# Attention placed between the gate tiles of the input projection, sample logits and values in four column quarters, raw input turned, last expert's rows summed over six banks

## The reference

```python
h = rmsnorm(x, norm1_g)
z = h @ w_in      # u | q | k | v | indexer q, k, weights | gate_pool | gate_attn
pool_out = pool_mix(concat(pool_hist, u))          # windows 2, 4, 8, 16, then w_pool
q, k = rmsnorm(q, q_norm_g), rmsnorm(k, k_norm_g)
att = dsa_attention(q, qi, wi, k_all, v_all, ik_all)   # top keys by an indexer, bias, softmax
mixed = sigmoid(g_pool) * (pool_out @ w_branch_pool) + sigmoid(g_attn) * (att @ w_branch_attn)
x = x + mixed @ w_out
x = x + moe_ffn(rmsnorm(x, norm2_g))   # top 4 of 32 experts, clamped SwiGLU, 12.6 MB of weights each
```

## Time and profile before

| | |
|---|---|
| median of 3 runs | 1384.34 us (1380.25 to 1384.99) |
| the profiled execution | 1380.85 us, span 1379.0 us |
| PE busy | 1310.8 us, 95% |
| DVE, ACT, POOL busy | 430.8, 189.9, 34.4 us |
| moved by DMA | 443.14 MB, mean 321 GB/s |

### The profile page before, as it was taken

One profiled execution on the slowest core, in us unless ns is written; L12 is line 12 of the kernel. 1 busy time (PEld: TensorE's weight loads), 2 busy tenths in 40 slices (PEclk: granted clock), 3 DMA queues, 4 the chain that ended last, 5 costly groups with the idle time before them and its releaser, 6 DMA issues.

```text
span 1379.0 us, 15153 instructions
## 1 busy us (share of the span) xinstructions
PE 1310.8 (95%) x6011; PEld 578.0 (42%) x6011; DVE 430.8 (31%) x779; ACT 189.9 (14%) x361; POOL 34.4 (2%) x37
## 2 busy tenths in 40 slices
PE   5999997789899999999999999999999999999996
PEld 2435444765455434344343443434434344343422
DVE  1047004132143343322433223332233323333223
ACT  3121112230111110101101111011110101101000
POOL 4000004000000000000000000000000000000000
PEclk9999999889998999999999999999999999999998
DMA  9131231031626999999999999999999999999993
GB/s 320 62 122 62 95 120 63 1 130 62 261 102 239 367 428 429 428 428 429 428 428 430 427 429 430 426 430 429 427 430 429 427 429 429 428 430 428 428 430 135
DMA packets 45716, 443.14 MB, mean 321 GB/s; under 512 B 4931, under 2 KB 6747, under 8 KB 20606
## 3 DMA queue, kind: packets, MB, share of 16 engines
q1 hardware_dynamic: 41344, 434.93, 75.6%
q10 hardware_dynamic: 3054, 4.90, 1.0%
q0 software_dynamic: 1296, 2.99, 0.7%
HBM read 439.27 MB, written 3.53 MB: 321 GB/s over the span
## 4 chain that ended last, share of the span: by engine, by line
PE 77%; DMA 3%; DVE 2%; ACT 1%; issue 0%; SPq 0%; DVEq 0%; POOL 0%; PEldq 0%
PE bank L1494 33%; PE bank L1505 16%; PE bank L1514 7%; PE bank L1480 7%; PE bank L1351 3%; PE bank L1432 3%; PE bank L1556 2%; DMA ring<-in_w_down 2%; PE bank L1569 1%; DMA wpool<-in_w_pool 1%; PE bank L1363 1%; PE bank L1362 1%; PE bank L1333 1%; PE bank L1332 1%; DMA ring<-in_w_out 1%; ACT logit L614 1%
## 5 line engine op out<-in xcount | busy, mean ns | idle before, releaser
L1494 PE MATMUL bank<-ring,xT 128*64 128x512 f32 x2048 | 475.2, 600 | 1.0 <-DVE xT L1057 0.7
L1494 PEld LDWEIGHTS bank<-ring,xT 128*64 128x64 f32 x2048 | 132.8, 136 | 285.0 <-issue 278.4
L1505 PE MATMUL bank<-ring,aT 128*64 128x512 f32 x1024 | 227.7, 597 | 2.4 <-DMA ring<-in_w_down 2.4
L1081 DVE TENSOR_TENSOR x<-x,bank 128x512 f32<-128x512 f32 x198 | 127.2, 684 | 129.1 <-PE bank L1514 129.1
L1161 PE MATMUL bank<-ring,hT 128*128 128x512 f32 (+1 forms) x384 | 161.9, 582 | 2.2 <-DMA ring<-in_w_in 1.9
L1505 PEld LDWEIGHTS bank<-ring,aT 128*64 128x64 f32 x1024 | 72.4, 138 | 143.1 <-issue 138.6
L1514 PE MATMUL bank<-yS,back 64*128 64x512 f32 x396 | 112.8, 646 | 8.4 <-DVE x L1081 7.6
L1094 DVE TENSOR_TENSOR gz<-bank,bguT 128x512 f32<-128x512 f32 x64 | 41.2, 686 | 221.8 <-PE bank L1556 221.8
L1161 PEld LDWEIGHTS bank<-ring,hT 128*128 128x128 f32 x384 | 73.5, 193 | 86.8 <-issue 82.8
L1480 PEld LDWEIGHTS bank<-pick,h 128*128 128x128 f32 x768 | 88.8, 195 | 13.2 <-issue 13.2
L1480 PE MATMUL bank<-pick,h 128*128 128x128 f32 x768 | 91.8, 281 | 1.0 <-DVE pick L1013 1.0
(11 more groups left out here) (253 smaller groups left out, 783.4 us busy)
## 6 DMA issues: line engine op xcount, KB each, us to landing
ring<-in_w_gate_up SPq DMA_DIRECT2D x128, 2048.0 KB, 17.3
ring<-in_w_down SPq DMA_DIRECT2D x64, 2048.0 KB, 17.3
ring<-in_w_in SPq DMA_DIRECT2D x16, 1024.0 KB, 8.1
ring<-in_w_out SPq DMA_DIRECT2D x4, 1024.0 KB, 5.9
ring<-in_cache_k SPq DMA_DIRECT2D x2, 1024.0 KB, 6.7
ring<-in_cache_v SPq DMA_DIRECT2D x2, 1024.0 KB, 6.7
ring<-in_w_branch_pool SPq DMA_DIRECT2D x2, 1024.0 KB, 6.8
ring<-in_w_branch_attn SPq DMA_DIRECT2D x2, 1024.0 KB, 11.2
```

The costliest lines, as they stand in the source:

```text
L1081: V.tensor_tensor(x[:, t, 512 * h:512 * h + 512], x[:, t, 512 * h:512 * h + 512], bank[6 + h][:, :], ALU.add).then_inc(y_added, 1)
L1494: last = T.matmul(bank[j][64 * r:64 * r + 64, :], xT[:, w, SLOTS * a:SLOTS * a + SLOTS], src[:, FF * r + 512 * j:FF * r + 512 * j + 512], ...
L1505: last = T.matmul(bank[4][64 * r:64 * r + 64, :], aT[:, c, :], src[:, o:o + 512], start=(c == 0), stop=(c == KC - 1))
```

## The change

1. **Start.** SP issues the loads of x, the constants and then the weights, without waiting for x. POOL's loads wait for the first two weight units. PE turns the raw x; DVE multiplies by `norm1_g` while it copies `hT` out, and the inverse root is applied by ACT as the scale of each copy of a projection's sums. The first block runs in two halves of the contraction.
2. **Order.** Only the five blocks that feed the attention run as blocks (`DENSE`). The four gate blocks become twelve `gate_tile(k)`, one token tile each, in banks 6 and 7, and PE's list puts them between the steps of the attention. The ring's units are reordered to match; the stores of the new keys and values move from ACT's list to SP's. Gate columns are copied out plainly, and three Sigmoids over 2048 columns follow at the end.
3. **Samples.** `qblk` holds 32 columns per sample and head pair. Four matmuls with 32 columns each write rows 32c to 32c+31 of the bank. Values have turned probabilities (32 columns) as stationary operand and 128 columns of values as moving one, again four column quarters. Softmax's division moves behind the values (`rowS`), whose rows are then turned back (8 transposes).
4. **End.** The last expert's gates are turned in the middle of the expert before's `down`, its places ahead, and the rows of the last two experts are summed for all three token tiles in six banks, so that x is added to once. x is stored in three parts.

```diff
-            sp.wait_ge(x_in[NT - 1], 16)
+            for t in range(NT):
+                src = I["x_prompt"][0, t * P:(t + 1) * P, :] if t < 2 else I["x_sample"].rearrange("b s d -> (b s) d")
+                sp.dma_start(x[:, t, :], src).then_inc(x_in[t], 16)
...
+            pool.wait_ge(unit_in[0], 16)
+            pool.wait_ge(unit_in[1], 16)
...
-            pe.wait_ge(xn_ready, NT)
-            for c in range(KC):
-                for t in range(NT):
-                    last = T.transpose(bank[c][:, t * P:(t + 1) * P], xn[:, t, c::KC], ident)
+            for m in range(2 * NT):
+                t, hf = divmod(m, 2)
+                pe.wait_ge(x_in[t], 16)
+                for q in range(4):
+                    last = T.transpose(bank[m][:, q * P:(q + 1) * P], x[:, t, 4 * hf + q::KC], ident)
...
                 for m in range(4):
-                    out = bank[2 * r + m // 2]
+                    b = 4 * r + m
+                    out = bank[((4, 0), (1, 2))[r][m // 2]]
                     o = (m % 2) * 256
-
-                    T.matmul(out[:, o:o + 256], rep[:, 4 * r + m, :], neg[:, 2, :], start=True, stop=False)
+                    T.matmul(out[:, o:o + 256], rep[:, b, :], neg[:, 2, :], start=True, stop=False)
                     for c in range(PAIRS):
-                        T.matmul(out[:, o:o + P], qblk[:, m, c, :], kTs[:, m, c, :], start=False, stop=False)
-                        last = T.matmul(out[:, o + P:o + 256], qblk[:, m, c, :], kT[:, c, 2 * P:], start=False,
-                                        stop=(c == PAIRS - 1))
+                        T.matmul(out[32 * c:32 * c + 32, o:o + P], qblk[:, b, c, :], kTs[:, m, c, :], start=False, stop=False)
+                    for c in range(PAIRS):
+                        last = T.matmul(out[32 * c:32 * c + 32, o + P:o + 256], qblk[:, b, c, :], kT[:, c, 2 * P:],
+                                        start=False, stop=True)
...
+                        for own in range(2):
+                            for c in range(PAIRS):
+                                v = zv[:, 2, c * P:(c + 1) * P] if own else ring[:, (vc_u + r) % RING, m * 512 + c * P:m * 512 + (c + 1) * P]
+                                last = T.matmul(bank[4 + r][32 * c:32 * c + 32, m * P:(m + 1) * P],
+                                                pT[:, 2 * b + own, 32 * c:32 * c + 32], v, start=(own == 0), stop=(own == 1))
...
                     for w in range(4):
-                        down(place + (KC if more else 0) + w, i, w)
+                        if final and w == 2:
+                            pe.wait_ge(z_added, 2 * n + 2)
+                            turn_gates(n + 1)
+                        down(place + KC + w, i, w)
...
+            for t in range(NT):
+                combine_last(t, back, True)
+            pe.wait_ge(at_ready, n + 1)
+            for w in range(4):
+                down(KC + UNITS + w, turns, w, aT2)
+            pe.wait_ge(y_out, n + 2)
+            pe.wait_ge(back_ready, n + 2)
+            for t in range(NT):
+                combine_last(t, back2, False)
```

More of the change, by code:

```diff
@@ L502, in _ @@
             act.wait_ge(sumsq_done, NT)
+            act.wait_ge(root_set, 1)
             A.activation(rsx, ssx, ACT.Sqrt, bias=eps, scale=1.0 / D).then_inc(rms_done, 1)
[L505 to L512, removed]
+            act.wait_ge(rsx_ready, 1)
             def z_block(m):
@@ L730, in turn @@
             def turn(i, final):
-                for a in range(2):
+                for a in range(1 if final else 2):
                     n = 2 * i + a
@@ L750, in _ @@
             turn(turns, True)
+            units = turns * (2 * UNITS) + KC
+            sigmoid(turns * 2 + 2)
+            rows_out(units + UNITS)
+            act.wait_ge(back_turned, turns * 2 + 2)
+            A.activation(back2[:], bank[5][:, 0:TOK].rearrange("p (t q) -> p t q", t=NT), ACT.Copy).then_inc(back_ready, 1)
+            rows_out(units + (UNITS + 4))
         @block.vector
@@ L1165, in z_block @@
                 pe.sem_inc(released, 2)
-            z_block(0)
+            pe.wait_ge(ht_ready, 2 * NT)
+            for half in range(2):
+                unit_wait(pe, half)
+                for t in range(NT):
+                    for c in range(4 * half, 4 * half + 4):
+                        last = z_part(0, t, c)
+                    if half:
+                        last.then_inc(z_done, 1)
+            pe.wait_ge(z_done, NT)
+            pe.sem_inc(released, 2)
+            pe.wait_ge(relb_in, 32)
+            T.matmul(bank[6][0:H, 0:NREL], relb[:], onehot[:], start=True, stop=True).then_inc(pe_small, 1)
             pe.wait_ge(idx_in, 16)
@@ new lines, in turn_rows_back @@
+            def turn_rows_back():
+                for bb in range(2):
+                    pe.wait_ge(rows_ready, bb + 1)
+                    for m in range(4):
+                        last = T.transpose(bank[4 + bb][:, m * P:(m + 1) * P], rowS[:, 4 * bb + m, :], ident)
+                    last.then_inc(rows_turned, 1)
+            turn_heads(0)
+            gate_tile(0)
+            turn_heads(4)
+            gate_tile(1)
+            logits(0)
+            gate_tile(2)
+            turn_probs(0)
@@ new lines, in _ @@
+            logits(1)
+            gate_tile(3)
+            values(0)
+            gate_tile(4)
+            turn_probs(1)
+            gate_tile(5)
+            values(1)
+            turn_keys(0)
+            gate_tile(6)
+            cache_logits(0)
+            turn_keys(1)
+            gate_tile(7)
+            cache_logits(1)
+            gate_tile(8)
+            gate_tile(9)
+            turn_probs(2)
+            gate_tile(10)
+            cache_values()
+            pool_mix()
+            gate_tile(11)
```

552 lines of the change are left out of this document (298 added, 254 removed).

## The result

The changed kernel takes 1312.39 us (median of 4, 1310.48 to 1315.62) where the one before takes 1383.32: a ratio of 0.9501, interval 0.9485 to 0.9517. The forecast was 1313. The two profiled executions (1380.85 us before, 1315.62 after) lie at opposite ends of their kernels' runs, so their spans differ by 65.2 us only.

| from | to | before | after | gained | forecast |
|---|---|---|---|---|---|
| start | pool rows turned | 153.3 | 144.4 | 8.9 | 10 |
| there | last branch matmul | 201.6 | 154.7 | 46.9 | 50 |
| there | first `gate_up` | 73.0 | 73.5 | -0.5 | 0 |
| there | first wait for the last `w_down` is over | 911.6 | 913.1 | -1.5 | 0 |
| there | end | 39.5 | 28.1 | 11.4 | 11 |

The account below looks back on a forecast made before the run. PE, 95% busy, was taken as the bound, with PE and DMA limits together in the experts. Start 10, attention 50 and end 11 sum to 71: 1384.3 - 71 = 1313 us, range 1306 to 1320, chance 0.62.

Parts of the forecast that it names:

- Start, 10 us forecast: Kernel start: first block begins at 11.0 instead of 21.54 us, less 0.5 for the `rel_bias` matmul; 10 us gained.
- the second of the two times that were worked out: First block: turned x, with DVE's last copies, ready at 10.9 us; the other time, the weights', was 11.0.
- Attention, 50 forecast: Pool rows turned to end of branch matmuls: 201.6 us becomes 151.3, gate tiles covering the softmax; 50 us less.
- the gate tiles: Attention: twelve tiles, nine at 6.9 us (a third of a block) and three at 4.4, make 75.3 us.
- waits move: Rival: ACT, DVE or queues come late for some gate tiles, half of 22.5 us idle stays; 1324 us, chance 0.15.
- the halves were the right neighbour: Samples' matmuls: quarters behave as halves do, four run beside each other, so eight matmuls take 0.44 us.
- Starts: Rival, samples: starts at 0.068 us set the pace, a sample's 16 take 1.09 instead of 0.44; 1323 us, chance 0.10.
- no overlap: Rival, samples: quarters do not run beside each other, 1.74 us instead of 0.44; 1334 us, chance 0.06.
- the slower case: Rival, samples: every change of quarter empties the array, 128 matmuls at 0.78 us; 1406 us, chance 0.02.
- the estimate of 3.2: Samples: speed-up of four column tiles, estimated from the skill's 2.38 for three; a round 0.55 us, sum 1.7 longer.
- End, 11 forecast: Last two experts to the end: finish at 1367.5 in a span of 1379.0; 11 us, 7 if additions wait as before.
- the gain reaches the end: Expert stage moves forward whole; rival, transfers set the experts' pace and only the end's 11 us stay: 1373, chance 0.03.

Follow-up runs that it names:

- one_quarter: Changed kernel with half of the samples' quarter matmuls writing rows 0 to 31, so it computes another thing; 2261.45 us, including a second pass over the experts.
- quarter_runs: Changed kernel with the samples' two matmuls that write one quarter listed one behind the other, then the next quarter; 1311.16 us, 0.9486 of the kernel before.
- old_end: Changed kernel with all of the end as in the kernel before; 1325.59 us, 0.9585 of the kernel before.
- late_gates: Changed kernel with the last expert's gates turned behind the whole `down` of the expert before, not in its middle; 1317.04 us, 0.9523 of the kernel before.
- gates_first: Changed kernel with the first six gate tiles ahead of the attention instead of between its steps; 1334.59 us, 0.9660 of the kernel before.
- mended: Changed kernel with second logits earlier, sample masks paired, gated rows turned early and w_out begun on the weight units there; 1303.25 us, 0.9440 of the kernel before.

## Why the prediction was right

**Start, 10 us forecast, 8.9 in the pair of traces.** The block began at 12.0, not 11.0; it waited for DVE's last copy of the turned x, which is the second of the two times that were worked out, about 1 us later than that. Over the traces the u rows begin to turn at 138.6 to 142.5 (before: 150.7), 8.2 to 12.1 earlier. By the runs POOL's hold carries 5.6 us of it; the early issue isn't told from scatter. No run takes away the turning of the raw x, and it matters as well: by the earlier trace rows PE ended the transposes of `xn` at 13.38 + 4.62 = 18.0, so with `xn` as before the block could not have begun at 12.0, however early the weights came.

**Attention, 50 forecast, 46.9.** The pieces came out as summed: the samples' logits 9.4 (forecast 9.5), values with their end 4.0 (3.7), the branch matmuls 41.4 (41.2), logits and values of the prompt 6.0 (6.0). The term that was sized too small is the gate tiles: the twelve fill 77.0 us, not 75.3. They were costed as thirds of a block; a tile with other work behind it ends 0.1 to 0.3 later. Transposes made 12.0 instead of 11.4, waits 2.2 instead of 1.6. Beyond the 0.9 us that was counted, no wait for ACT appeared, and none for a weight unit or a queue, so "waits move" fell; that the tiles hide the softmax was shown by taking them away.

**Quarters.** Four beside each other, 0.22 for eight instructions, against 8 x 0.109 = 0.87 on one quarter: the halves were the right neighbour. "Starts" (1.09 for 16) and "no overlap" (1.74) fell with the period of 1.20 us, and so did the slower case, a drain at each change. That case was priced from masks that ran at full pace (0.21 us from one instruction of 256 columns to the next), so its price held no slow clock, though its words had one. The earlier trace rows shown as 0.07 us are a weak reading against starts 0.062 or 0.068 apart; a view of 0.02 us (224.01 to 224.03) still holds both starts, which settles it. The Trainium skill, TensorE: Matmul & The Clock Gate, Part 3, gives 2.38 for three column tiles at 512 columns. Here a sample's 16 instructions take 0.44 us on four quarters, and they would take 16 x 0.109 = 1.74 on one by the spacing in `one_quarter`, four times that; so the measurement decides against the estimate of 3.2. The same part of the Trainium skill says that matmuls start strictly in program order. The records of `quarter_runs` and `one_quarter` show otherwise for column quarters in fp32.

**End, 11 forecast, 11.4** in the pair and 12.1 by `old_end`. The places of the gain are the forecast ones; `late_gates` shows that the place of the turned gates carries 4.3 of it, more than the 1.2 that were counted there.

**The rest.** The two stages that were to stay lost 2.0 us together, in one trace. With 65.2 the traces give less than the 71 summed, and the medians 70.9. Of the gap of 5.7, 2.5 is that the profiled execution of before lies so far under its median, and 2.3 may be the slow first block (23.20 against 20.87), which most traces do not have; the last microsecond stays open. That the median came within 1 us is therefore luck in part; terms of 10, 50 and 11 that were each within 13% of what the traces show (8.9, 46.9 and 11.4) are not. That the gain reaches the end was shown three times: by the result, by `gates_first` and by `mended`, with 909 to 912 us from the first to the last `gate_up` in every trace but that of `one_quarter`.

## What to carry to other kernels

Independent work that stands in large blocks on the bounding engine was worth more here between the steps of a chain that waits for other engines: split it by the length of the waits (here 8.5 and 11.8 us, covered by tiles of 7), and count for each piece what a block pays once at its end (0.1 to 0.3 us). Before a step is moved, walk through the list of every engine that it passes: the price of `late_gates` lay in ACT's list, behind a Sigmoid. Matmuls with 32 output rows belong on different column quarters, and the width should be left as seldom as possible (4.71 us for four samples' logits with four changes to the full width, 4.04 with two).

## What was not expected of the hardware

The order of matmuls on different quarters in the program did not matter within a sample's 16 instructions: with two matmuls of one quarter one behind the other, the trace still shows four starts close together, then four more, at the same 0.22 to 0.24 us for eight. It doesn't name the quarters, but starts on one quarter lie 0.11 us apart in `one_quarter`, so four that lie close are on four quarters. With ten instructions of one quarter in a row the order did matter (`one_quarter`, where other quarters stood idle for 0.68 us). And the first microseconds of PE are slower than the clock's column says. The window over 12 to 17 us of the changed kernel:

```profile
12.00:17.00 5.00, 5.00 (x6) 2.18 (x7) 0.02 (x1) 0.00 (x0) 2.19 (x4) 1.00 1.05 387
```

The same window of `quarter_runs`:

```profile
12.00:17.00 5.00, 5.00 (x13) 2.25 (x12) 0.00 (x0) 0.00 (x0) 2.51 (x4) 1.00 1.05 387
```

Both print a clock of 1.00, but the first holds six instructions of 512 columns, most of them 0.85 us apart, and the second thirteen, 0.43 apart: the lower of the two levels (1.2 GHz) and the upper (2.4). What PE did before differs by the wait for the second tile of x, 0.78 us and 0.22.
